# Two widths of product in one: the weights of nineteen groups meet both parts of the activations at once

## What is computed

```python
# first block
p = u @ w_in + b_in                       # aq ak av hq hf hi hg gate_a gate_b
y_attn = sliding_window_sink_attention(aq, ak, av, sinks)
q, k = silu(hq), (1 - lb) * sigmoid(-hf)  # log_f = log(lb + (1 - lb) * sigmoid(hf))
o = hgrn2_chunkwise(q, k, hi, log_f)      # 8 heads of 128, chunks of 64
y_hgrn = rms(o) * norm_g * sigmoid(hg)
merged = sigmoid(gate_a) * (y_attn @ w_branch_attn) + sigmoid(gate_b) * (y_hgrn @ w_branch_hgrn)
h = x + merged @ w_out
...
# second block
z, xbc, dt, q, k, v = split(h2 @ w_in_2)
y_ssd = ssd_mixer(z, xbc, dt, ...)        # gated by silu(z)
y_att = chunk_attention(q, k, v, rel_bias)
```

## Time and profile before

| | before |
|---|---|
| median of 3 runs | 816.12 us (815.12 to 816.71) |
| the profiled execution | 815.34 us, its span 813.6 us |
| TensorE busy | 796.6 us, 5952 products |
| weight loads | 5952 |
| VectorE busy | 592.4 us |
| ScalarE busy | 498.6 us |
| granted TensorE clock, mean | 0.998 |

### The profile page before, as it was taken

One profiled execution on the slowest core, in us unless ns is written; L12 is line 12 of the kernel. 1 busy time (PEld: TensorE's weight loads), 2 busy tenths in 40 slices (PEclk: granted clock), 3 DMA queues, 4 the chain that ended last, 5 costly groups with the idle time before them and its releaser, 6 DMA issues. The chain is left out here.

```text
span 813.6 us, 14276 instructions
## 1 busy us (share of the span) xinstructions
PE 796.6 (98%) x5952; PEld 744.8 (92%) x5952; DVE 592.4 (73%) x772; ACT 498.6 (61%) x752; POOL 15.8 (2%) x36
## 2 busy tenths in 40 slices
PE   8999999999999999999999999999999999999996
PEld 8988879999999889999998889999788999999885
DVE  5575686648766877887878897897768877787463
ACT  6777788568837475344344266856657776666452
POOL 3000000000200000000000000000000000000000
PEclk9999999999999999999999999999999999999999
DMA  8873634446453577889798993635352865646611
GB/s 301 285 252 111 207 104 156 155 155 226 162 183 105 160 254 232 264 292 298 253 300 279 354 358 110 234 133 155 104 173 68 256 205 168 197 137 200 233 52 52
DMA packets 105680, 161.15 MB, mean 198 GB/s; under 512 B 4480, under 2 KB 51856, under 8 KB 105616
## 3 DMA queue, kind: packets, MB, share of 16 engines
q1 hardware_dynamic: 105472, 159.97, 59.8%
q10 hardware_dynamic: 144, 0.26, 0.1%
HBM read 159.16 MB, written 1.06 MB: 197 GB/s over the span
## 5 line engine op out<-in xcount | busy, mean ns | idle before, releaser
L1073 DVE TENSOR_TENSOR wL<-raw,wH 128x2048 fp32r<-128x2048 f32 (+2 forms) x134 | 283.0, 2118 | 122.7 <-ACT wH L695 119.2
L1672 PE MATMUL ps<-p1H,wH 128*128 128x256 f32 x1256 | 359.2, 286 | 1.7 <-DVE p1L L1073 0.8
L1672 PE MATMUL ps<-p1L,wH 128*128 128x256 f32 x1256 | 355.3, 283 | 0.0
L1672 PE MATMUL ps<-p1H,wL 128*128 128x256 f32 x1256 | 355.3, 283 | 0.0
L695 ACT ACTIVATE wH<-raw 128x2048 fp32r<-128x2048 f32 (+1 forms) x120 | 223.1, 1866 | 122.1 <-PE ps L1672 65.9
L1672 PEld LDWEIGHTS ps<-p1H,wH 128*128 128x128 f32 x1256 | 240.8, 192 | 4.8 <-issue 3.5
L1672 PEld LDWEIGHTS ps<-p1L,wH 128*128 128x128 f32 x1256 | 240.9, 192 | 0.3 <-issue 0.2
L1672 PEld LDWEIGHTS ps<-p1H,wL 128*128 128x128 f32 x1256 | 240.8, 192 | 0.0
L1675 PE MATMUL ps<-wH,zH 128*128 128x512 f32 x168 | 65.4, 389 | 0.0
L1675 PE MATMUL ps<-wH,zL 128*128 128x512 f32 x168 | 65.4, 389 | 0.0
L1675 PE MATMUL ps<-wL,zH 128*128 128x512 f32 x168 | 65.4, 389 | 0.0
(11 more groups left out here) (284 smaller groups left out, 974.5 us busy)
## 6 DMA issues: line engine op xcount, KB each, us to landing
raw<-in_w_in SPq DMA_DIRECT2D x37, 1024.0 KB, 5.1
raw<-in_w_ada SPq DMA_DIRECT2D x24, 1024.0 KB, 5.2
raw<-in_w_up SPq DMA_DIRECT2D x44, 512.0 KB, 4.8
raw<-in_w_ffn_gate SPq DMA_DIRECT2D x22, 512.0 KB, 4.5
raw<-in_w_ffn_up SPq DMA_DIRECT2D x22, 512.0 KB, 5.6
raw<-in_w_ffn_down SPq DMA_DIRECT2D x10, 1024.0 KB, 5.3
raw<-in_w_down SPq DMA_DIRECT2D x10, 1024.0 KB, 5.0
raw<-in_w_out SPq DMA_DIRECT2D x8, 1024.0 KB, 5.1
```

The source lines that it names most:

```text
L1073: return v.tensor_tensor(o, a, b, op)
L1672: last = mm(ps[:, t[1], 0:T], wt[:, slot, k, t[2]:t[2] + P], at_[:, k0 + k, :], start=st, stop=en)
```

## The change

In nineteen "cm" groups (q, hq, hf, hg, ga, gb, ba, bh, each 0 and 1, and z, q2, k2) the activation's high and low part lie side by side in one buffer, so that `wH` meets both in one product of 512 columns; `wL` meets the high part in a second of 256. A tile now fills its bank: the left half holds H x H + L x H, the right half H x L. The halves have to be added:

- q0, q1, q2, k2: ScalarE applies bias or scale to the right half (`first`), VectorE adds the left half (`add`).
- hq, hf, hg, ga, gb, z: VectorE folds both halves with a TENSOR_REDUCE into SBUF (`fold`); ScalarE applies its functions to that, in place for most (`second`).
- ba, bh: VectorE folds into `brow` (`folded`), then multiplies from there. As `brow` is in use longer, SyncE loads the gate bias into it after the merge instead of after hi1.

`evac` of all nineteen now counts on VectorE ("DDDD").

```diff
-        GROUPS[f"{_name}{_i}"] = group("w_in", [(_c + _i * W, W)], cm_tiles(4 * _i if _name in ("q", "hf", "hg") else 0), "AAAA", "P1")
+        GROUPS[f"{_name}{_i}"] = group("w_in", [(_c + _i * W, W)], cm_tiles(4 * _i if _name in ("q", "hf", "hg") else 0), "DDDD", "P1")
...
+WIDE = {f"{_n}{_i}" for _n in ("q", "hq", "hf", "hg", "ga", "gb", "ba", "bh") for _i in range(2)} | {"z", "q2", "k2"}
...
-        p1H = sb("p1H", [P, KD, T], F32R)
-        p1L = sb("p1L", [P, KD, T], F32R)
+        p1 = sb("p1", [P, KD, 2, T], F32R)
+        p1H, p1L = p1[:, :, 0], p1[:, :, 1]
...
-                    sp.wait_ge(*EV["hi1", 1])
+                    sp.wait_ge(on.merged, KD)
...
+                def first(dst, f, scale=1.0, b0=None):
+                    for m, t in enumerate(GROUPS[name]["tiles"]):
+                        act.wait_ge(on.tile_done, TILE[name, m])
+                        nc.scalar.activation(dst(m), ps[:, t[1], T:2 * T], f, scale=scale,
+                                             bias=0.0 if b0 is None else pc("b_in", b0 + 4 * i + m)).then_inc(on.sig_part, 1)
+                def second(buf, f, b0=None):
+                    for m in range(4):
+                        act.wait_ge(*EV[name, m])
+                        ins = nc.scalar.activation(buf(m), buf(m), f,
+                                                   bias=0.0 if b0 is None else pc("b_in", b0 + 4 * i + m))
...
                 elif g == "hf":
-                    act.wait_ge(on.hq_done, i + 1)
...
                     for m in range(4):
-                        act.wait_ge(on.tile_done, TILE[name, m])
-                        nc.scalar.activation(T1[:, m], ps[:, 4 * i + m, 0:T], ACT.Sigmoid,
-                                             bias=pc("b_in", 18 + 4 * i + m)).then_inc(on.sig_part, 1)
...
+                        act.wait_ge(*EV[name, m])
+                        nc.scalar.activation(T2[:, m], T1[:, m], ACT.Sigmoid, scale=-1.0,
+                                             bias=negb[:, 4 * i + m:4 * i + m + 1])
+                        nc.scalar.activation(T1[:, m], T1[:, m], ACT.Sigmoid,
                                              bias=pc("b_in", 18 + 4 * i + m)).then_inc(on.sig_part, 1)
...
+                def add(dst, scale=None):
+                    for m, t in enumerate(GROUPS[name]["tiles"]):
+                        dve.wait_ge(*passed(name, m))
+                        if scale is None:
+                            tt(dst(m), ps[:, t[1], 0:T], dst(m), ALU.add).then_inc(on.evac_dve, 1)
...
+                def folded(dst, m):
+                    dve.wait_ge(on.tile_done, TILE[name, m])
+                    o = ps[:, GROUPS[name]["tiles"][m][1], :].rearrange("p (a n) -> p n a", a=2)
+                    return v.tensor_reduce(dst, o, AX_X, ALU.add)
...
                 elif g == "ba":
                     for m in range(4):
-                        dve.wait_ge(on.tile_done, TILE[name, m])
-                        tt(GA[:, 4 * i + m], ps[:, m, 0:T], GA[:, 4 * i + m], ALU.mult).then_inc(on.evac_dve, 1)
+                        o = brow[:, wide(m)]
...
+                        step(folded(o, m))
+                        tt(GA[:, 4 * i + m], o, GA[:, 4 * i + m], ALU.mult).then_inc(on.evac_dve, 1)
...
+                    if name in WIDE:
+                        cs = slice(t[2], t[2] + P)
+                        mm(ps[:, t[1], :], wH[:, slot, k, cs], BOTH[g["act"]][:, k0 + k].rearrange("p a n -> p (a n)"),
+                           start=part == 0 and k == 0, stop=False)
+                        return mm(ps[:, t[1], 0:T], wL[:, slot, k, cs], aH[:, k0 + k, :], start=False,
+                                  stop=final and k == nk - 1)
```

More of the change, by code:

```diff
@@ L75 @@
 for _name, _c in (("z", 0), ("xs", 512), ("bc", 1024), ("q2", 1544), ("k2", 2056)):
-    GROUPS[_name] = group("w_in_2", [(_c, W)], cm_tiles(), "AAAA", "P1")
+    GROUPS[_name] = group("w_in_2", [(_c, W)], cm_tiles(), "DDDD" if _name in ("z", "q2", "k2") else "AAAA", "P1")
 GROUPS["v2"] = group("w_in_2", [(2568, W)], tm_tiles(0, W), "AA", "P1")
+WIDE = {f"{_n}{_i}" for _n in ("q", "hq", "hf", "hg", "ga", "gb", "ba", "bh") for _i in range(2)} | {"z", "q2", "k2"}
+PASSES = ("q0", "q1", "hq0", "hf0", "hq1", "hf1", "q2", "z", "k2")
 UNITS = [(1, 0, 0, 8, 1), (1, 0, 8, 8, 1), (1, 1, 0, 4, 2), (1, 1, 4, 4, 2), (1, 1, 8, 4, 2), (1, 1, 12, 4, 2),
@@ L409, in at @@
             return nc.alloc_sbuf_tensor_at(name, shape, dt, offset=base + kb * 1024)
-        pyH = at("pyH", 0, [P, KD, T], F32R)
-        pyL = at("pyL", 8, [P, KD, T], F32R)
+        py = at("py", 0, [P, KD, 2, T], F32R)
+        pyH, pyL = py[:, :, 0], py[:, :, 1]
         zH = at("zH", 0, [P, KF, T], F32R)
@@ L820, in each @@
                             nc.scalar.activation(dst(m), ps[:, t[1], 0:T], f, **bias).then_inc(on.evac_act, 1)
-                if g == "q" and name in ("q0", "q1"):
-                    each(lambda m: aQ[:, 4 * i + m], ACT.Identity, bias=lambda m: pc("b_in", 4 * i + m))
+                def first(dst, f, scale=1.0, b0=None):
[8 more added lines that the diff above has]
+                                                   bias=0.0 if b0 is None else pc("b_in", b0 + 4 * i + m))
+                        if name in PASSES:
+                            ins.then_inc(on.sig_part, 1)
+                if name in ("q0", "q1"):
+                    first(lambda m: aQ[:, 4 * i + m], ACT.Identity, b0=0)
                 elif name == "kv":
@@ L830, in evac @@
                 elif g in ("ga", "gb"):
-                    b0, G = (42, GA) if g == "ga" else (50, GB)
-                    each(lambda m: G[:, 4 * i + m], ACT.Sigmoid, bias=lambda m: pc("b_in", b0 + 4 * i + m))
+                    b1, G = (42, GA) if g == "ga" else (50, GB)
+                    second(lambda m: G[:, 4 * i + m], ACT.Sigmoid, b1)
                 elif g == "hq":
-                    act.wait_ge(on.ext_out, 16)
-                    if i:
-                        act.wait_ge(on.o_psum, 2 * i)
@@ L837, in evac @@
                     for m in range(4):
[L838 to L839 removed]
+                        act.wait_ge(*EV[name, m])
+                        nc.scalar.activation(SQ[i][:, m], hQ[:, m], ACT.Sigmoid, bias=pc("b_in", 10 + 4 * i + m))
+                        nc.scalar.activation(hQ[:, m], hQ[:, m], ACT.Identity,
                                              bias=pc("b_in", 10 + 4 * i + m)).then_inc(on.sig_part, 1)
[L841 to L842 removed]
@@ L856, in evac @@
-                    each(lambda m: hG[:, m], ACT.Sigmoid, bias=lambda m: pc("b_in", 34 + 4 * i + m))
+                    second(lambda m: hG[:, m], ACT.Sigmoid, 34)
                 elif g == "f":
@@ L868, in evac @@
                 elif name == "q2":
-                    each(lambda m: turned(q2[:, m]), ACT.Copy, scale=0.125)
+                    first(lambda m: turned(q2[:, m]), ACT.Copy, 0.125)
                 elif name == "k2":
-                    each(lambda m: k2[:, m], ACT.Copy)
+                    first(lambda m: k2[:, m], ACT.Copy)
                 elif name == "z":
-                    each(lambda m: sZ[:, m], ACT.Silu)
+                    second(lambda m: sZ[:, m], ACT.Silu)
                 elif name == "v2":
```

57 lines of the change are left out of this document (41 added, 16 removed).

## The result

| | before | after |
|---|---|---|
| median | 816.13 us (815.12 to 816.71, 4 runs) | 849.38 us (848.88 to 850.54, 4 runs) |
| ratio, 95% interval | | 1.0411 (1.0393 to 1.0429) |
| profiled execution, its span | 815.34 us, 813.6 us | 849.36 us, 847.6 us |
| mean granted clock of TensorE | 0.998 | 0.979 |

A forecast was written before the change was run, and what follows sets the result against it. The prediction took TensorE's own product spacing as the bound, except in the attention panels, where a ScalarE and VectorE chain ends last. Terms 6.1 + 19.5 - 0.8 + 1 = +25.8 us on 815.3 gave 841 us, range 822 to 858.

The forecast's parts named there:

- The gain: On TensorE, pairing saves a fixed 13 ns for each of 608 triples of products, 7.9 us.
- The fold: On VectorE, 60 added folds of 0.69 us each, bounds 0.42 and 1.22.
- Attention: From 42 to 137 us, folds queued behind VectorE's weight split delay the chain to the transposes: +6.1 us.
- Second HGRN half: From 176 to 223 us, folds and passes in hq1, hf1 and hg1 run in series: +12.6 us before matrix A.
- ba, bh, out: Folds delay splits that bh0 and out0's second panel need: +3.1 and +4.4 us, with 0.3 given back.
- q2, z, k2: Folds are covered by the panels; six panels gain 1.25 us, last additions before the scores take 0.45: -0.8 us.
- The clock: The 6.4 us pause before matrix A may lower TensorE's granted clock: +1 us, between 0 and 4.
- Rival (a): Faster: the queues have slack at every named place, decided at matrix A, only 7.9 us gained: 807 us; 10%.
- (b): Attention alone: HGRN absorbs the folds, the attention's loss stays: 818 us; 7%.
- (d): A product's fixed part grows with its columns, so pairing saves 2.5 ns, not 13: 845 us; 3%.
- the signs: TensorE waits 20 to 30 us for VectorE, 6 at matrix A; folds 0.69 us; VectorE some 640 us.
- I am wrong: If TensorE waits under 10 us in all, folds take over 0.9 us, or pairs are not 0.347 us apart.

The follow-up runs named there:

- left_half: Changed kernel's wide products kept, but emptied as in the kernel before, from the left half of the bank alone, nothing folded: 812.96 us, ratio 0.9961.
- all_early: Changed kernel with the four folds ahead of the final panel's wL split in hq1, hf1, hg1, ga0, ga1, hq0, hf0 and hg0: 836.09 us, ratio 1.0243.
- gaps: Kernel before the change, with four waits put into TensorE's queue in quiet feed-forward stages (f2, f7, u2, u7): 835.27 us, ratio 1.0219.
- filled: Changed kernel with idle products on TensorE while it waits before out0's second panel and before matrix A: 846.87 us, ratio 1.0366.
- attn_apart: Changed kernel with ga0, ga1, hq0, hf0 and hg0 back on the old products and emptying: 841.25 us, ratio 1.0301.
- h1_early: Changed kernel with the four folds ahead of the final panel's wL split in hq1, hf1 and hg1 only: 841.5 us, ratio 1.0307.
- ba_bh_apart: Changed kernel with ba0, ba1, bh0 and bh1 back on the old products and emptying: 840.35 us, ratio 1.0283.
- fold_twice: Changed kernel with the four folds of gb1 and of hg1 done twice each: 850.43 us, ratio 1.0426.

## Why the prediction was right, and where not

849.4 lies in the range (822 to 858), 8 us above the forecast of 841, and the likeliest case is the one that came. 0.8 of the 8 are the base: the terms were added to the profiled execution (815.3) and the result is a median. That the range held is in part luck. Its upper end stood on slower folds and on chained starts, but the folds took 0.68 us and the chains less than their sum; what filled that room was the clock, which passed its own bound of 4 us by 7.5. The terms:

- **The gain** (7.9 us from 608 x 13 ns) was mis-sized. Between pairs the products stand as the earlier trace rows say in places, but not everywhere. Here is TensorE after, in ga0's first panel and in hg0's:

```profile
43.90 0.28 PE L1733 MATMUL ps<-p,wL 128*128 128x256 f32 x1
...
46.38 0.28 PE L1733 MATMUL ps<-p,wL 128*128 128x256 f32 x1
...
131.07 0.28 PE L1733 MATMUL ps<-p,wL 128*128 128x256 f32 x1
...
133.50 0.28 PE L1733 MATMUL ps<-p,wL 128*128 128x256 f32 x1
```

  Seven pairs each: 0.354 us in the first, 0.347 in the second. left_half, the run that isolates it, gives 3.5 us in all by its trace, 3.2 by its ratio (1.9 to 4.5). The Trainium skill's 2.5 ns (TensorE: Matmul & The Clock Gate, section "Wait — 56ns, not 53.3ns?") would be 1.5 us, an estimate; the ratio's interval leaves that out, and what was measured lies between the page and my reading.
- **The fold** (0.69 us, 60 of them): 0.680 to 0.684. Right. Also the total of VectorE, 635 against 640.
- **Attention** (+6.1): the shift behind it is 7.0, of which 3.2 are the slow clock (the panels at 68.5 and 104.5 and the transposes of 102.88), so 3.8 by the prediction's own mechanism. TensorE waited 2.7, 2.8 and 2.2 us at three of the attention's transposes and 0.4 to 0.7 at the other three, not 2.5 to 3.5 at each. The delay per link was a little smaller than I made it, and all_early shows that its cause was the split ahead of the folds, as argued.
- **Second HGRN half** (+12.6 before matrix A): matrix A starts 19.4 us later than in the earlier trace rows, 12.5 of them since gb1; 1.5 of these are a slow panel, so 11.0. The waits came where the steps had them: 6.2 us at A (6.4 predicted), 3.8 at hg1's panels (5.6), 1.1 at hi1 (1.7).
- **ba, bh, out** (+3.1 - 0.3 + 4.4): 12.2 measured, of it 5.1 in the two slow panels, so 7.1 against 7.2.
- **q2, z, k2** (-0.8): +0.2. The panels won 0.4 and the last additions before the scores took 0.65 back.
- **The clock** (+1, between 0 and 4): **this step failed.** I had asked only whether the 6.4 us before matrix A would bring the clock down. They did, for 1.7 us; but five shorter waits, of 2 to 5 us, did so too and cost 9.8. The length of a wait does not give its price to a microsecond: the changed kernel lost 2.7 us behind the wait at bh0, where six other kernels with such a wait lost 1.3 to 1.4. gaps shows the price by itself, and filled that idle time is what is paid for.

Together: 3.8 + 11.0 + 7.1 + 0.2 + 11.5 = 33.6 us, against 33.4 by the panels' shift at the end. The clock term was 10.5 us too small; the queues' terms, 24.8 predicted, were 22.1. Rival (a) failed at the point it named, hK's 0.9 us of slack. Of (b) the opposite is true: HGRN absorbed nothing, and attn_apart prices the attention at 8.1 us of the 33.3. (d), a smaller gain from pairing, was true in its direction: the gain was 4.4 us less than the 7.9 predicted, not 6.4. Of the signs, 29 us of waiting for VectorE (20 to 30 expected), 6.2 of it at matrix A, came true; one of those that were to say "I am wrong" came true in part, as the pair is 0.347 us apart in some panels only.

What was not tried: the folds of ba and bh in another order against hsplit and the merge, so for those 9 us the runs show which groups make them, not that the order does; the rows say that VectorE's pyL split of bh0 and p1L split of out0 stood behind the folds.

## What to carry to other kernels

Before moving work to an engine with a free quarter of its time, look at what stands ahead of and behind it in that engine's queue and who waits there: four more folds cost nothing behind gb1 and their full 2.9 us behind hg1. Where an emptying has to move to the engine that also prepares the weights, put it ahead of the preparation that is due two panels later; here that alone gave back 13 us of 33, the clock's share with it, and still left the change a loss. And price each new TensorE wait of some 3 us at half as much again, for the slow clock behind it, or fill it with products that nobody needs.

## What the runs showed of the hardware

- The mean granted clock fell from 0.998 to 0.979, about 16 us' worth of cycles in a span of 847.6 (0.019 of it); 11.5 us of it show as slower work, the rest fell into waits. The Trainium skill (TensorE: Matmul & The Clock Gate, section "Part 1: The HAM clock gate (the "warmup" mystery)") has the low clock as the idle state, which activity releases. The rows agree: in gaps the clock was 0.77, 0.66 and 0.80 over the panels behind the three longer waits and had been 0.5 for a part of each, and it was back at 1.00 while products ran. The Trainium skill (same page, section "Terms") has the penalty as the throttled time by one minus the ratio; here that sum is an upper bound, since a slow clock cost nothing while TensorE waited anyway.
- In gaps a wait of 1.3 us had no slow stretch behind it, waits of 2.7 us had one of 1.3 to 1.6 us' cost, one of 5.3 us cost 2.6. Which wait is hit varies between kernels that hardly differ there: the attention's slow panels moved between variants, bh0's wait of 2.9 us had none behind it in filled, and seven of the eleven experiments (left_half, h1_early, attn_apart, ba_bh_apart, fold_twice, filled and gaps) had one at xs, behind small products and short waits (0.15 us in left_half), where the kernel before and the changed one had none. So the clock's part of such a result is good to some 2 us at best.
- A pair of a 512- and a 256-column product took 0.347 us on the mean in some panels and 0.354 in others (single pairs 0.343 to 0.361), while three 256-column ones took 0.360. What decides it stays open.
